# Square sums of a differential-attention entry: from 32 small TensorE products over eight tiles to sums on GpSimd and VectorE and 8 products

## The chip, the cores and the metric

One Trainium2 chip, one core. The metric is the device time of one execution in microseconds, the median of several runs. The core's engines work side by side and meet at semaphores: TensorE (PE in the profile, its weight loads PEld), VectorE (DVE), ScalarE (ACT), GpSimd (POOL) and SyncE (SP), which issues the transfers here.

## What is computed

Two transformer blocks of different kinds run one after the other on 512 tokens of width 1024, all in float32. The first ends in a norm, the second begins with one, and a differential attention follows:

```python
def rms_norm(x, g):
    y = xf * lax.rsqrt(jnp.mean(xf * xf, axis=-1, keepdims=True) + EPS)
    return (y * g.astype(jnp.float32)).astype(x.dtype)
...
    return rms_norm(x, final_norm)            # end of the first block
...
def rms_norm_2(x, g=None):                    # start of the second block
...
def diff_attention(h, w_in, q_g, k_g, ...):
    proj = h @ w_in
    q, k, v = jnp.split(proj, [2 * H * d, 4 * H * d], axis=-1)
    q = apply_partial_rope(rms_norm_2(q.reshape(B, S, 2 * H, d), q_g), cos, sin) * (d ** -0.5)
    k = apply_partial_rope(rms_norm_2(k.reshape(B, S, 2 * H, d), k_g), cos, sin)
...
```

The two norms in a row need two sums for each token: of x squared, and of (x times `final_norm`) squared. From them come two factors for each token: one by which the residual is scaled (first norm alone) and one for the rows of `h @ w_in` (both norms).

## The kernel before

Activations lie feature-major: `xT` is 8 tiles of 128 features x 512 tokens. Every large product is made of three float32r matmuls (`mm3`): weights and activations are each split into a high and a low part (`whi`, `wlo`; `hh`, `hl`), and high x high, high x low and low x high are added. Weights arrive in blocks of 128 x 2048 through three buffers. SyncE loads a block when TensorE has used the one three before it (`s_used`), ScalarE makes its high part (L952), GpSimd its low part in four instructions (`split_to`, L759).

Four engines run hand-written queues; their order is the order of the code. At the **entry** of the differential attention (stage `diff`, first block number b), for each tile t VectorE adds the last down-projection from PSUM to `xT` (L2362), ScalarE writes `hh` (L981, gain folded in) and the squares `a_xsq[:, t, :]` (L984), and VectorE writes `hl` (L2380). TensorE meanwhile works through the input projection with the tokens as rows: block b first (4 contraction tiles x 4 row tiles), then `half_group(b + 1, 0, 1, (0, 1))` and `half_group(b + 1, 0, 1, (2, 3))`, which finish group 0 of the rows. A half group of two row tiles is 24 large matmuls.

Before the change, TensorE also makes the token sums. `half_group` takes a function `between` that it calls ahead of each contraction tile; `squares` there issues 4 products of 2 columns, 32 in all, with a tile of `a_xsq` as the stationary operand and `gsq[:, t, :]` (ones, and the squared `final_norm`) as the moving one. The sums land in PSUM bank 7 with tokens on partitions. After the last one (`s_ess`) VectorE computes the factors `dr` (L2765 to L2772, with two ScalarE instructions for the inverse root between), and `s_rr` lets ScalarE copy group 0's rows out of PSUM (L1219, L1220).

The residual's factor is also needed as a row, the same on all partitions (`rstd`). For this VectorE builds four diagonal matrices (L2775) in `sq`, TensorE multiplies them by ones (L1951) in bank 6, and VectorE copies the result (L2792). That copy stands in VectorE's queue behind group 0's norm and rotation, and TensorE waits for it (`s_fcopy`) and for the rotated rows (`s_rows`) ahead of `turn_rows`, the 16 transposes of group 0 (L1901), which use banks 4 to 7.

## Time and profile before

| | us |
|---|---|
| median of 3 runs | 2386.46 |
| lowest, highest run | 2382.07, 2394.81 |
| span of the profiled execution | 2382.2 |
| TensorE busy | 2355.2 (99%) |
| GpSimd busy | 1162.4 (49%) |
| ScalarE busy | 853.5 (36%) |
| VectorE busy | 798.0 (33%) |

The profiled execution has no time of its own beside its span, which agrees with the fastest run to 0.1 us. TensorE's busy time is modelled for pipelined matmuls: a large matmul of 512 columns is shown as 0.39 us, though the next one starts 0.23 us after it. So starts are compared with starts below. A float32 product appears as two records, a float32r product or a transpose as one. An idle time in brackets names what ended it.

### The profile page before, as it was taken

The page shows a single profiled execution, that of the slowest core. Times are in us where ns is not written, and L with a number is a line of the kernel's source. Part 1 is how long each engine was busy: PE and PEld are TensorE (multiplying, and loading weights), DVE is VectorE, ACT ScalarE, POOL GpSimd, SP SyncE. Part 2 cuts the span into 40 slices and gives each one's busy share as a digit, 9 for nine tenths or more (in the row PEclk, how much of TensorE's full clock was granted, in tenths as well). Part 3 has the DMA queues.
Part 4 walks back from the last instruction along what each step waited for, and adds up shares of the span by engine and source line. Part 5 has one row for each costly group of instructions (what it writes and reads, how often), then busy time and mean ns, then how long its engine had stood idle before and what let it go on. Part 6 is the DMA issues. An engine that isn't in the chain of part 4 may idle for free.

```text
span 2382.2 us, 27151 instructions
## 1 busy us (share of the span) xinstructions
PE 2355.2 (99%) x11234; PEld 1924.9 (81%) x11234; DVE 798.0 (33%) x1384; ACT 853.5 (36%) x1266; POOL 1162.4 (49%) x960
## 2 busy tenths in 40 slices
PE   8999999999999999999999999999999999999999
PEld 7888887888887788888887678888887777788887
DVE  3222205854212322100466742022046863410210
ACT  4222214514342322212446543223156463431330
POOL 6544446634554544444452365444556822644443
PEclk9999999999999999999999999999999999999999
DMA  4323233212332323232220122233232201322322
GB/s 147 106 89 105 89 100 113 89 54 71 124 122 67 95 89 106 89 106 89 85 92 19 54 89 91 104 90 105 89 103 67 75 1 54 94 102 91 96 96 89
DMA packets 147521, 210.54 MB, mean 88 GB/s; under 512 B 6203, under 2 KB 113862, under 8 KB 147398
## 3 DMA queue, kind: packets, MB, share of 16 engines
q1 hardware_dynamic: 147398, 208.80, 27.2%
q8 instruction: 89, 1.46, 0.2%
q14 instruction: 34, 0.28, 0.0%
HBM read 206.69 MB, written 2.10 MB: 88 GB/s over the span
## 4 chain that ended last, share of the span: by engine, by line
PE 88%; DVE 7%; issue 2%; POOL 1%; DMA 1%; ACT 1%; SPq 0%; DVEq 0%; POOLq 0%; ACTq 0%
PE ps L1465 27%; PE ps L1467 26%; PE ps L1466 26%; PE ps L2243 2%; DVE c_work L2964 1%; DVE c_best L2963 1%; DVE small L2807 1%; PE ps L2221 1%; POOL wlo L759 1%; PE ps L2231 1%; PE ps L1726 1%; PE ps L1794 1%; POOL sq L774 1%; PE ps L1816 1%; DVE hl L2380 1%
## 5 line engine op out<-in xcount | busy, mean ns | idle before, releaser
L759 POOL TENSOR_TENSOR wlo<-raw,whi 128x512 fp32r<-128x512 f32 x776 | 1007.0, 1329 | 1082.9 <-ACT whi L952 981.8
L952 ACT ACTIVATE whi<-raw 128x2048 fp32r<-128x2048 f32 (+1 forms) x185 | 352.4, 1905 | 688.2 <-DMA raw<-in_mlp_w 317.1
L1465 PE MATMUL ps<-hh,whi 128*128 128x512 f32 x1448 | 572.9, 396 | 6.6 <-DVE hl L2380 5.4
L1467 PE MATMUL ps<-hh,wlo 128*128 128x512 f32 x1448 | 566.3, 391 | 0.0
L1466 PE MATMUL ps<-hl,whi 128*128 128x512 f32 x1448 | 566.3, 391 | 0.0
L1465 PEld LDWEIGHTS ps<-hh,whi 128*128 128x128 f32 x1448 | 273.5, 189 | 73.1 <-issue 9.3
L1467 PEld LDWEIGHTS ps<-hh,wlo 128*128 128x128 f32 x1448 | 273.3, 189 | 57.7
L1466 PEld LDWEIGHTS ps<-hl,whi 128*128 128x128 f32 x1448 | 273.7, 189 | 56.8 <-issue 1.2
L1466 PE MATMUL ps<-gl,whi 128*128 128x512 f32 x736 | 286.4, 389 | 0.0
L1465 PE MATMUL ps<-gh,whi 128*128 128x512 f32 x736 | 286.3, 389 | 0.0
L1467 PE MATMUL ps<-gh,wlo 128*128 128x512 f32 x736 | 286.3, 389 | 0.0
L2362 DVE SCALAR_TENSOR_TENSOR xT<-ps,xT 128x512 f32<-128x512 f32 x72 | 49.0, 684 | 479.3 <-PE ps L1467 479.3
L1466 PEld LDWEIGHTS ps<-gl,whi 128*128 128x128 f32 x736 | 138.1, 188 | 28.7
L1465 PEld LDWEIGHTS ps<-gh,whi 128*128 128x128 f32 x736 | 138.1, 188 | 28.7
L1467 PEld LDWEIGHTS ps<-gh,wlo 128*128 128x128 f32 x736 | 138.1, 188 | 28.6
L1465 PE MATMUL ps<-whi,hh 128*128 128x512 f32 (+2 forms) x408 | 154.5, 379 | 0.2 <-POOL wlo L759 0.2
L1467 PE MATMUL ps<-whi,hl 128*128 128x512 f32 (+2 forms) x408 | 151.4, 371 | 0.0
L1466 PE MATMUL ps<-wlo,hh 128*128 128x512 f32 (+2 forms) x408 | 151.3, 371 | 0.0
L2432 DVE SCALAR_TENSOR_TENSOR ps<-ps,rstd 128x512 f32<-128x512 f32 x64 | 41.5, 694 | 196.4 <-PE ps L1467 196.4
L1024 ACT ACTIVATE ps<-ps 128x512 f32<-128x512 f32 x64 | 37.1, 583 | 150.4 <-DVE ps L2432 150.0
L2417 DVE TENSOR_TENSOR ps<-ps,sg 128x512 f32<-128x512 f32 x44 | 28.5, 694 | 186.5 <-PE ps L1467 186.3
L1465 PEld LDWEIGHTS ps<-whi,hh 128*128 128x128 f32 x408 | 76.8, 188 | 14.5 <-POOL wlo L759 1.2
(448 smaller groups left out, 2920.1 us busy)
## 6 DMA issues: line engine op xcount, KB each, us to landing
raw<-in_mlp_w SPq DMA_DIRECT2D x64, 1024.0 KB, 5.5
raw<-in_ffn_w_up SPq DMA_DIRECT2D x22, 1024.0 KB, 5.1
raw<-in_ffn_w_down SPq DMA_DIRECT2D x22, 1024.0 KB, 4.8
raw<-in_ffn_w_gate SPq DMA_DIRECT2D x21, 1024.0 KB, 5.1
raw<-in_w_in SPq DMA_DIRECT2D x13, 1024.0 KB, 5.1
raw<-in_diff_w_in SPq DMA_DIRECT2D x12, 1024.0 KB, 5.0
raw<-in_xattn_w_kv SPq DMA_DIRECT2D x8, 1024.0 KB, 5.2
raw<-in_dsa_w_in SPq DMA_DIRECT2D x8, 1024.0 KB, 5.0
```

Of the source, the lines that this page charges most:

```text
L759: nc.gpsimd.tensor_tensor(wlo[i][:, c], raw[i][:, c], whi[i][:, c].bitcast(F32), ALU.subtract).then_inc(s_lo, 1)
L774: nc.gpsimd.tensor_tensor(sq[:, 0, :], first, sg[:, t % 4, :], ALU.add).then_inc(s_eacc, 1)
L952: nc.scalar.activation(whi[i][:, 0:width(made[0])], raw[i][:, 0:width(made[0])], ACT.Copy)\
L1024: nc.scalar.activation(ps[:, bank + n, :], ps[:, bank + n, :], ACT.Square)\
L1465: nc.tensor.matmul(dst, w_hi, x_hi, start=start, stop=False)
L1466: nc.tensor.matmul(dst, w_hi, x_lo, start=False, stop=False)
L1467: return nc.tensor.matmul(dst, w_lo, x_hi, start=False, stop=stop)
L1726: r = nc.tensor.matmul(ps[:, bank, ts(n, CH)], m_state[rows, d, h // 2, n, :], m_qin[rows, d, h // 2, ts(n, CH)], start=False, stop=d == 1 ...
L2243: r = nc.tensor.matmul(ps[:, 6, c:c + 64], c_pT[:, 2 * (p % 2) + a, ts(kb, P)], a_v[:, kb, ts(2 * j + a, 64)], start=kb == 0, stop=kb == qt)
L2362: V.scalar_tensor_tensor(out=xT[:, n, :], in0=ps[:, n, :], scalar=scale, in1=xT[:, n, :], op0=ALU.mult, op1=ALU.add).then_inc(s_x, 1)
L2417: dv.done(V.tensor_tensor(ps[:, bank + 2 + n, :], ps[:, bank + 2 + n, :], sg[:, (k0 + n) % 4, :], ALU.mult))
L2432: V.scalar_tensor_tensor(out=ps[:, bank + n, :], in0=ps[:, bank + n, :], scalar=0.0, in1=rstd[:, :], op0=ALU.max, op1=ALU.mult).then_inc(s ...
```

## The change

- GpSimd adds the eight tiles of `a_xsq` into `sq[:, 0, :]` with seven instructions, between its work on block b+1 and on block b+2.
- VectorE adds the same tiles, each times the squared gain of its features, into `sq[:, 1, :]` with eight instructions, each of which waits for the one before.
- `gsq` holds the squared gains alone, and `acc_at`, by which later entries count GpSimd's adds, counts the new seven too.
- TensorE waits for both and makes 8 products of 2 columns (4 row tiles x 2 sums) between the two half groups of block b+1, in place of the 32 inside the first one.
- The factor row comes from four TensorE transposes of a column of `dr`, broadcast along the free dimension, placed between block b+2 and block b+3. The four diagonals and the product with ones go away. VectorE's copy and TensorE's wait for it stay.

```diff
         def acc_at(e):
-            return 7 * (e - (e > E_DIFF))
+            return 7 * e
...
             def diff(b):
+                split_to(b + 1)
+                for t in range(1, KT):
+                    pool.wait_ge(s_esq, 8 * E_DIFF + t + 1)
+                    if t > 1:
+                        pool.wait_ge(s_eacc, acc_at(E_DIFF) + t - 1)
+                    first = a_xsq[:, 0, :] if t == 1 else sq[:, 0, :]
+                    nc.gpsimd.tensor_tensor(sq[:, 0, :], first, a_xsq[:, t, :], ALU.add).then_inc(s_eacc, 1)
                 split_to(b + DIFF_BLOCKS - 1)
...
                 pe.wait_ge(s_el, 8 * E_DIFF + 8)
-                pe.wait_ge(s_esq, 8 * E_DIFF + 8)
                 pe.wait_ge(s_x, x0 + 8)
-
-                def squares(st, k):
-
-                    row, part = divmod(4 * st + k, 2)
-                    for t in range(4 * part, 4 * part + 4):
-                        r = nc.tensor.matmul(ps[:, 7, 2 * row:2 * row + 2], a_xsq[:, t, ts(row, P)], gsq[:, t, :],
-                                             start=t == 0, stop=t == KT - 1)
-                    if row == ST - 1 and part:
-                        r.then_inc(s_ess, 1)
-
-                half_group(b + 1, 0, 1, (0, 1), squares)
+                half_group(b + 1, 0, 1, (0, 1))
+                pe.wait_ge(s_eacc, acc_at(E_DIFF) + 7)
+                pe.wait_ge(s_fsq, 1)
+                for st in range(ST):
+                    for n in range(2):
+                        r = nc.tensor.matmul(ps[:, 7, 4 * st + 2 * n:4 * st + 2 * n + 2], sq[:, n, ts(st, P)],
+                                             ones[:, 0:2], start=True, stop=True)
+                r.then_inc(s_ess, 1)
                 half_group(b + 1, 0, 1, (2, 3))
...
                 for g in range(1, 5):
                     half_group(b + 2 * g, 4 * g, 0)
+                    if g == 1:
+                        pe.wait_ge(s_rr, 1)
+                        for st in range(ST):
+                            r = nc.tensor.transpose(ps[:, 6, ts(st, P)], dr[:, st:st + 1].broadcast_to([P, P]),
+                                                    ident[:, :])
+                        r.then_inc(s_frow, 1)
                     half_group(b + 2 * g + 1, 4 * g, 1, (0, 1))
                     if g == 1:
-                        pe.wait_ge(s_fdiag, 4)
-                        nc.tensor.matmul(ps[:, 6, :], ones[:, :], sq[:, 0, :], start=True, stop=True)\
-                            .then_inc(s_frow, 1)
                         pe.wait_ge(s_fcopy, 1)
...
             def diff(b, upd, down):
+                for t in range(KT):
+                    dve.wait_ge(s_esq, 8 * E_DIFF + t + 1)
+                    if t == 0:
+                        last = V.tensor_scalar(sq[:, 1, :], a_xsq[:, 0, :], gsq[:, 0:1], None, ALU.mult)
+                    else:
+                        last = V.scalar_tensor_tensor(out=sq[:, 1, :], in0=a_xsq[:, t, :], scalar=gsq[:, t:t + 1],
+                                                      in1=sq[:, 1, :], op0=ALU.mult, op1=ALU.add)
+                    if t < KT - 1:
+                        dv.link(last)
+                last.then_inc(s_fsq, 1)
                 dve.wait_ge(s_ess, E_DIFF + 1)
...
-                dve.wait_ge(s_rr, 1)
-                for st in range(ST):
-                    V.tensor_scalar(sq[:, 0, ts(st, P)], ident[:, :], dr[:, st:st + 1], None, ALU.mult)\
-                        .then_inc(s_fdiag, 1)
```

TensorE at the end of block b and the start of b+1, before the change (`hh`, `hl` stationary or moving as the row says; `whi`, `wlo` the weights' parts, the number is the buffer's):

```order
L1467 MATMUL ps<-whi_58,hl 128x512
L1924 MATMUL ps<-gsq,a_xsq 128x2 [waits s_x,s_lo,s_esq,s_el]
L1924 MATMUL ps<-gsq,a_xsq 128x2 x3
L1465 MATMUL ps<-whi_59,hh 128x512
L1466 MATMUL ps<-wlo_56,hh 128x512
L1467 MATMUL ps<-whi_59,hl 128x512
L1924 MATMUL ps<-gsq,a_xsq 128x2 x4
```

The small products now stand together, 24 large matmuls later, between the halves of b+1 (`ones` is the moving operand):

```order
L1472 MATMUL ps<-whi_59,hh 128x512
L1473 MATMUL ps<-wlo_56,hh 128x512
L1474 MATMUL ps<-whi_59,hl 128x512
L1930 MATMUL ps<-ones,sq 128x2 [waits s_fsq,s_eacc]
L1930 MATMUL ps<-ones,sq 128x2 x7
L1472 MATMUL ps<-whi_59,hh 128x512 [waits s_lo]
```

They wait for two sums that were not there before, and the second half of b+1 stands behind them.

VectorE, from the end of the entry to the head sums of group 0, before:

```order
L2362 SCALAR_TENSOR_TENSOR xT<-ps,xT 128x512 [waits s_used]
L2380 SCALAR_TENSOR_TENSOR hl<-xT,g_90,hh 128x512 [waits s_eh] x2
L2765 TENSOR_SCALAR dr<-ps 128x4 [waits s_ess]
L2766 TENSOR_SCALAR newton<-ps 128x4
L2767 SCALAR_TENSOR_TENSOR dr<-dr,newton 128x4 [waits s_dv]
L2770 TENSOR_TENSOR newton<-dr 128x8 [waits s_erstd]
L2771 TENSOR_TENSOR dr<-dr,newton 128x8 [waits s_dv]
L2772 SCALAR_TENSOR_TENSOR dr<-dr 128x8 [waits s_dv]
L2775 TENSOR_SCALAR sq<-ident,dr 128x128 [waits s_rr]
L2775 TENSOR_SCALAR sq<-ident,dr 128x128 x3
L2757 TENSOR_REDUCE small<-a_sq 128x32 [waits s_rcopy,s_dv,s_rope]
```

And now:

```order
L2368 SCALAR_TENSOR_TENSOR xT<-ps,xT 128x512 [waits s_used]
L2386 SCALAR_TENSOR_TENSOR hl<-xT,g_90,hh 128x512 [waits s_eh] x2
L2771 TENSOR_SCALAR sq<-a_xsq,gsq 128x512 [waits s_esq]
L2773 SCALAR_TENSOR_TENSOR sq<-a_xsq,gsq,sq 128x512 [waits s_esq,s_dv] x7
L2780 TENSOR_SCALAR dr<-ps 128x4 [waits s_ess]
L2781 TENSOR_SCALAR newton<-ps 128x4
L2782 SCALAR_TENSOR_TENSOR dr<-dr,newton 128x4 [waits s_dv]
L2785 TENSOR_TENSOR newton<-dr 128x8 [waits s_erstd]
L2786 TENSOR_TENSOR dr<-dr,newton 128x8 [waits s_dv]
L2787 SCALAR_TENSOR_TENSOR dr<-dr 128x8 [waits s_dv]
L2762 TENSOR_REDUCE small<-a_sq 128x32 [waits s_rcopy,s_dv,s_rope]
```

The eight sums have come in ahead of the factors, and the four diagonals behind them are gone. Since the file is a few lines longer, line numbers behind a point move: L2380 is L2386 in the changed kernel, L2765 is L2780.

GpSimd in the changed kernel, where before the rows of L759 followed each other without a break:

```order
L759 TENSOR_TENSOR wlo_56<-raw_53,whi_59 128x512 [waits s_hi]
L759 TENSOR_TENSOR wlo_56<-raw_53,whi_59 128x512 x3
L862 TENSOR_TENSOR sq<-a_xsq 128x512 [waits s_esq]
L862 TENSOR_TENSOR sq<-sq,a_xsq 128x512 [waits s_eacc,s_esq] x6
L759 TENSOR_TENSOR wlo_57<-raw_54,whi_60 128x512 [waits s_hi]
```

The seven adds stand ahead of the low parts of block b+2.

## Rows read from the trace of the kernel before

**Rows 1.** Page, busy us, share of the span and instructions of an engine.

```profile
PE 2355.2 (99%) x11234; PEld 1924.9 (81%) x11234; DVE 798.0 (33%) x1384; ACT 853.5 (36%) x1266; POOL 1162.4 (49%) x960
```

**Rows 2.** Timeline of TensorE at the first small products: start, us, instructions.

```profile
1143.38 0.95 PE L1924 MATMUL ps<-gsq,a_xsq 128*128 128x2 f32 x8
1144.19 0.49 PE L1465 MATMUL ps<-whi,hh 128*128 128x512 f32 x1
...
1144.99 0.95 PE L1924 MATMUL ps<-gsq,a_xsq 128*128 128x2 f32 x8
```

**Rows 3.** Timeline of TensorE from the last cluster to group 0's transposes.

```profile
1156.09 0.40 PE L1465 MATMUL ps<-whi,hh 128*128 128x512 f32 x1
...
1177.88 1.02 PE L1951 MATMUL ps<-sq,ones 128*128 128x512 f32 x2
1179.69 1.97 PE L1901 MATMUL ps<-ident,a_rows 128*128 128x128 f32 x16 [0.78 <-DVE rstd L2792]
1181.41 0.47 PE L1465 MATMUL ps<-whi,hh 128*128 128x512 f32 x1
```

**Rows 4.** Timeline of VectorE from the entry to the copy of the factor row.

```profile
1130.85 1.10 DVE L2380 SCALAR_TENSOR_TENSOR hl<-xT,g,hh 128x512 fp32r<-128x512 f32 x1 [5.67 <-ACT hh L981]
...
1139.66 1.62 DVE L2380 SCALAR_TENSOR_TENSOR hl<-xT,g,hh 128x512 fp32r<-128x512 f32 x2
1155.49 0.16 DVE L2765 TENSOR_SCALAR dr<-ps 128x4 f32<-128x4 f32 x1 [14.21 <-PE ps L1924]
...
1178.24 0.42 DVE L2754 TENSOR_TENSOR a_rows<-t 128x256 f32<-128x256 f32 x1
1178.94 0.69 DVE L2792 COPY rstd<-ps 128x512 f32<-128x512 f32 x1 [0.28 <-PE ps L1951]
```

**Rows 5.** Timeline of GpSimd beside it: low parts of b+1 and b+2.

```profile
1128.85 5.95 POOL L759 TENSOR_TENSOR wlo<-raw,whi 128x512 fp32r<-128x512 f32 x4 [5.99 <-ACT whi L952]
1142.89 4.98 POOL L759 TENSOR_TENSOR wlo<-raw,whi 128x512 fp32r<-128x512 f32 x4 [8.10 <-ACT whi L952]
```

**Rows 6.** Timeline of VectorE at the third MLP pass's entry, first and last `hl`.

```profile
2022.59 1.09 DVE L2380 SCALAR_TENSOR_TENSOR hl<-xT,params,hh 128x512 fp32r<-128x512 f32 x1 [10.30 <-ACT hh L981]
...
2032.71 2.88 DVE L2380 SCALAR_TENSOR_TENSOR hl<-xT,params,hh 128x512 fp32r<-128x512 f32 x2
```

**Rows 7.** Timeline of GpSimd at that entry: low parts, then adds.

```profile
2020.60 5.94 POOL L759 TENSOR_TENSOR wlo<-raw,whi 128x512 fp32r<-128x512 f32 x4 [7.15 <-ACT whi L952]
...
2028.38 9.79 POOL L774 TENSOR_TENSOR sq<-sq,sg 128x512 f32<-128x512 f32 x6
```

**Rows 8.** All instructions of line L2380: ns min/median/max.

```profile
L2380 DVE SCALAR_TENSOR_TENSOR hl<-xT,params,hh x48: 733/1180/1785, 7.4 to 2033.8; 128x512 fp32r<-128x512 f32 x48
```

**Rows 9.** Timeline of VectorE in the first block's convolution, GpSimd idle.

```profile
516.11 0.54 DVE L2611 TENSOR_SCALAR m_conv<-m_u,params 128x512 f32<-128x512 f32 x1
516.68 0.75 DVE L2612 SCALAR_TENSOR_TENSOR m_conv<-m_u,params,m_conv 128x511 f32<-128x511 f32 x1
517.47 0.75 DVE L2614 SCALAR_TENSOR_TENSOR m_conv<-m_u,params,m_conv 128x511 f32<-128x511 f32 x1
```

**Rows 10.** Timelines of VectorE and GpSimd in the cross-attention's factors.

```profile
623.25 1.21 DVE L2352 SCALAR_TENSOR_TENSOR xqr<-xqr 128x4 f32<-128x4 f32 x1
624.49 1.22 DVE L2701 TENSOR_SCALAR xqr<-xqr 128x4 f32<-128x4 f32 x1
...
620.66 5.03 POOL L759 TENSOR_TENSOR wlo<-raw,whi 128x512 fp32r<-128x512 f32 x4 [2.08 <-ACT whi L952]
```

**Rows 11.** TensorE behind a long wait: stretches (busy, granted clock, DMA share, GB/s), then timeline.

```profile
1404.00:1407.00 3.00, 2.92 (x7) 0.50 0.00 0
1404.00:1410.00 6.00, 5.92 (x20) 0.75 0.00 0
...
1404.08 0.80 PE L1465 MATMUL ps<-hh,whi 128*128 128x512 f32 x1 [3.31 <-DVE hl L2380]
1404.67 0.63 PE L1466 MATMUL ps<-hl,whi 128*128 128x512 f32 x1
1405.10 0.63 PE L1467 MATMUL ps<-hh,wlo 128*128 128x512 f32 x1
```

More of the change, by code:

```diff
@@ L259, in two_blocks @@
         g12 = const("g12", [P, KT])
-        gsq = const("gsq", [P, KT, 2])
+        gsq = const("gsq", [P, KT])
         c_best = const("c_best", [P, 8])
@@ L452, in two_blocks @@
         s_dny = sem("s_dny")
-        s_fdiag = sem("s_fdiag")
+        s_fsq = sem("s_fsq")
         s_frow = sem("s_frow")
@@ L2474, in tables @@
                 at12, at1 = PARAM_AT["norm_mix_2"], PARAM_AT["final_norm"]
-                dv.done(V.memset(gsq[:, :, 0], 1.0))
-                dv.done(V.tensor_tensor(gsq[:, :, 1], params[:, at1:at1 + KT], params[:, at1:at1 + KT], ALU.mult))
+                dv.done(V.tensor_tensor(gsq[:, :], params[:, at1:at1 + KT], params[:, at1:at1 + KT], ALU.mult))
                 dv.done(V.tensor_tensor(g12[:, :], params[:, at12:at12 + KT], params[:, at1:at1 + KT], ALU.mult))
@@ L2762, in diff @@
             def diff(b, upd, down):
+                for t in range(KT):
[8 more added lines that the diff above has]
+                last.then_inc(s_fsq, 1)
                 dve.wait_ge(s_ess, E_DIFF + 1)
                 y, w, u = dr[:, 0:8], dr[:, 8:16], newton[:, 1, 0:8]
-                dv.done(V.tensor_scalar(w[:, 0:4], ps[:, 7, 0:8:2], -0.5 / D, -0.5 * EPS, ALU.mult, ALU.add))
-                dv.link(V.tensor_scalar(u[:, 0:4], ps[:, 7, 1:8:2], -0.5 / D, None, ALU.mult))
+                dv.done(V.tensor_scalar(w[:, 0:4], ps[:, 7, 0:16:4], -0.5 / D, -0.5 * EPS, ALU.mult, ALU.add))
+                dv.link(V.tensor_scalar(u[:, 0:4], ps[:, 7, 2:16:4], -0.5 / D, None, ALU.mult))
                 V.scalar_tensor_tensor(out=w[:, 4:8], in0=w[:, 0:4], scalar=EPS, in1=u[:, 0:4],
```

## Prediction

> **What bounds the kernel now.** I read the page first: TensorE is busy for 2355.2 of 2382.2 us [rows 1], so nearly every microsecond of this kernel is a TensorE microsecond. The change touches some 60 us around 1140 us, so the next views are the timelines of each engine there. I call the start of the square-sum products' reader on VectorE (the first `dr` instruction, L2765) the **handover**; it is at 1155.49 in the profile of before [rows 4].
>
> TensorE before the handover [rows 2]: eight clusters, each of eight records on L1924, then three large matmuls. From one cluster's start to the next takes 1144.99 - 1143.38 = 1.61 us, on the mean of all eight (1156.09 - 1143.38) / 8 = 1.59; the three large matmuls alone take 3 x 0.227 = 0.68 us (0.227 is the step through the 96 large matmuls from 1156.09 to 1177.88 in [rows 3]: 21.79 / 96). The code issues 32 products, four a cluster; the 64 of the change's title are records, two to a product. So "64 to 8" is 32 to 8 products, or 64 to 16 records.
>
> After the handover TensorE has more work than it needs to cover the row factors, but one place ties it to VectorE [rows 3, 4]: at 1177.88 it runs the ones-by-diagonal product (two records), VectorE copies `rstd` at 1178.94, and only then the 16 transposes of group 0 start, at 1179.69. VectorE reached that copy just in time: its last rotation instruction began at 1178.24 and took 0.42 us, so the copy could have begun at about 1178.70. From the handover to 1178.70 VectorE runs a chain of its own (factors, head sums, norm, rotation) of 23.2 us that the change leaves alone. **So what the change is worth is not what it takes off TensorE, but how far it moves the handover, plus the 1178.94 - 1178.70 = 0.24 us at the end.**
>
> **The parts, one by one.**
>
> *Removed on TensorE.* The clusters: 8 x (1.59 - 0.68) = 7.3 us. The ones-by-diagonal product and the wait behind it: 1179.69 - 1177.88 = 1.81 us [rows 3]. Four diagonal builds on VectorE lay in idle time and are worth nothing.
>
> *Added on TensorE.* 16 small records, at the pace of before's (8 in 1144.19 - 1143.38 = 0.81 us [rows 2]): 1.62 us at full clock. Four transposes: 16 take 1181.41 - 1179.69 = 1.72 us [rows 3], so 0.43, and 0.1 to get back to large matmuls: 0.55 us. They are placed 24 large matmuls ahead of the tie and wait for nothing late. A TensorE-only sum would be -7.3 - 1.8 + 1.7 + 0.55 = -6.8 us. The Trainium skill's page "TensorE: Matmul & The Clock Gate" (section "PE-mode transpose") gives about 275 ns for one 128x128 transpose in a kernel, which would make the four an estimated 1.1 us and the sum -6.1. The trace has them follow each other every 0.11 us, and the measurement decides.
>
> *Added on GpSimd: seven adds* of 128x512 behind the low parts of block b+1. GpSimd is idle there from 1134.80 (1128.85 + 5.95) to 1142.89 [rows 5], but VectorE is not: it writes `hl` and `xT`. The trace has the same arrangement once more, at the entry of the third MLP pass, where GpSimd also goes from four low parts straight to seven adds [rows 6, 7]. Its low parts end 3.95 us after the first `hl` instruction (2020.60 + 5.94 against 2022.59), as here (1134.80 against 1130.85, where `hl` of this entry begins). There VectorE's entry lasts 2032.71 + 2.88 - 2022.59 = 13.00 us; here it ends at 1139.66 + 1.62 = 1141.28, 10.43 us after its start [rows 4]. With the adds beside it I expect 13.00, an end at **1143.85**. The reason is in [rows 8]: `hl` instructions take 733 ns at best and 1785 at worst. The wait of TensorE for `hl` grows from nothing to 0.5 us (1143.38 to 1143.9); that is covered by what follows. GpSimd's adds end there 2028.38 + 9.79 - 2022.59 = 15.6 us after the start, so about two of them are still to come when VectorE leaves its entry, and behind them the four low parts of block b+2, whose high part ScalarE has by then. These low parts move from 1142.89 to past 1147, but TensorE wants them only after the remaining half of block b+1: covered.
>
> *Added on VectorE: eight dependent instructions* over `a_xsq`, begun only after its entry, and TensorE waits for the last. This is the costliest term. Undisturbed, the row for the first (tensor_scalar, SBUF, 128x512) is 0.54 us and for the others 0.79 from start to start (516.68 to 517.47) [rows 9]. Beside GpSimd they are slower: while GpSimd ran four low parts from 620.66 to 625.69, VectorE instructions on 128x4 elements took 1.2 us each, a tensor_scalar among them [rows 10]. So a VectorE instruction waits until GpSimd's current one is through. For 128x512 with two SBUF inputs the worst `hl`, 1.785 us [rows 8], is the last of a pair of 2.88 in [rows 6], whose starts are 1.09 apart; with 0.08 of overlap and 0.04 for the dependence I take **1.75 us a step**. GpSimd has 2 adds + 4 low parts left, so six steps are slow and two free: 6 x 1.75 + 2 x 0.79 = **12.1 us**, an end at 1143.85 + 12.1 = 1155.95. Bounds: none slow, 0.58 + 7 x 0.79 = 6.1 us; all eight slow, 14.0 us.
>
> The Trainium skill ("SBUF — State Buffer", section "Who interferes with whom") says that a VectorE instruction with two SBUF inputs and a GpSimd instruction that reads SBUF exclude each other for the whole instruction. By that rule a step would be a whole GpSimd instruction and a whole own one, an estimated 1.26 + 0.75 = 2.0 us in place of 1.75, and the result 1.5 us later; I keep the row. The rule speaks against this change.
>
> *The new wait and the clock.* TensorE has done the first half of block b+1 at 1143.9 + 24 x 0.227 = 1149.4 and then waits for VectorE until 1156.0, 6.6 us; behind that wait stand the small products, then the whole queue of large ones. In the profile of before, TensorE waited 3.31 us ahead of 1404.08, and over 1404 to 1407 the granted clock was 0.50, its lower level of 1.2 GHz: large matmuls came every 0.43 us (1404.67 to 1405.10) in place of 0.227, a factor of 1.9 [rows 11]. So I take the 16 small records at the lower clock: 1.62 x 1.9 = 3.1 us. The handover is then at 1155.95 + 0.05 + 3.1 + 0.05 = 1159.15, against 1155.49: **+3.65 us**.
>
> *Is VectorE still the later one at the tie?* From its large matmuls' resumption TensorE has 96 of them and four transposes, 21.8 + 0.55 = 22.3 us; VectorE needs 1179.69 - 0.24 - 1155.49 = 23.96 from handover to first transpose. The slack of 1.65 us swallows a few more large matmuls at the lower clock (seven cost 7 x 0.2 = 1.4). So the handover decides, and of TensorE's own 6.8 us nothing arrives.
>
> **Sum:** +3.65 - 0.24 = +3.4 us. The profiled execution has a span of 2382.2 us and lies at the fastest of the three runs (2382.07); with the change it would be 2385.6. Against the median of 2386.46 this gives **2390**. About 0.5% (12 us) is what a measurement of this kernel can tell from no change, so this is "no change", on the slow side.
>
> **Rivals.**
>
> A. *VectorE's sums don't collide with GpSimd* (for: undisturbed rows [rows 9]; against: [rows 8, 10]). End of sums 1143.85 + 6.1 = 1149.95, TensorE hardly waits, 1.62 us of products, handover 1151.7: -3.8 - 0.24 = -4.0, 2382.5. If even the tie were no limit, the TensorE-only sum of -6.8 would give 2379.7.
>
> B. *The collision is heavier*: all eight steps slow, 14.0 us (for: GpSimd may itself be slowed and so be busy longer; against: its own rows give six instructions left, [rows 7]). Handover 1.9 us later: +5.3, 2392. The Trainium skill's rule on the shared port (above) comes out here too, by its estimate.
>
> C. *The clock holds up* although TensorE waits: products 1.5 us shorter, +1.9, 2388.4. Against it: [rows 11].
>
> D. *Slower than before, measurably*: the wait of 6.6 us sends the clock down and it stays down through the 96 large matmuls, each 0.2 us longer: 19.2 less the slack of 1.65, +3.4 more, 21 us, 2407. It decides from about 50 large matmuls at the lower clock. Against it: in [rows 11] the low stretch had ended within 3 us of TensorE's resumption, since the mean of 1404 to 1410 is 0.75.
>
> E. *The change does not do what it says*: it saves TensorE products, but these were a filler that ran while VectorE's later chain was what counted. This is half true in my forecast; in full (handover unchanged) it gives -0.24, 2386.
>
> **How the numbers follow.** Chances: forecast 0.45, B 0.17, A 0.17 (0.04 of it with the tie gone), C 0.10, E 0.06, D 0.05. A to B reach from 2382.5 to 2392; the runs of before alone spread from 2382 to 2395, so a median of a few can lie some 3 us off: 2380 to 2396 leaves out D and the edges. Faster by over 0.5% needs -12 us, which no case gives, only the spread: 0.03. Slower by over 0.5%: D and a little spread, 0.06. Within: 0.91.
>
> **What would show it.** In the profile of the changed kernel: `hl` instructions of this entry at about 1.18 us throughout; the eight sums on VectorE at 1.6 to 1.8 us while GpSimd is busy and 0.75 after; a wait of TensorE of 5 to 8 us ahead of the small products, put down to VectorE, the largest in the kernel; a granted clock near 0.5 right behind it; the handover at 1157 to 1161; transposes of group 0 released by the `rstd` copy, with a wait of up to 1.7 us ahead. I am wrong if the sums take 0.8 us each beside GpSimd, if the wait is under 3 us, or if the time between handover and first transpose is not about 24 us.

## The result, and the profile after

| | before | after |
|---|---|---|
| median | 2386.11 us | 2389.99 us |
| lowest to highest | 2381.81 to 2394.81 | 2385.11 to 2393.36 |
| runs | 20 | 20 |

The ratio of the times is 1.0017, with a 95% interval of 1.0011 to 1.0024: the changed kernel is 3.9 us slower, which is real by its interval and below the half per cent that I called a difference. The forecast was 2390. The span of the profiled execution is 2387.6 us (2382.2 before). A few executions in the experiments, of before among others, took from about 3000 to 13000 us; the ratios leave them out, and the only profile of the kernel "new sums alone" is one of these, so it has no milestones below.

The page of after, engines, which answers to [rows 1]:

```profile
PE 2354.3 (99%) x11188; PEld 1921.2 (80%) x11188; DVE 810.7 (34%) x1387; ACT 854.0 (36%) x1266; POOL 1172.5 (49%) x967
```

TensorE has 46 instructions and 0.9 us of busy time less, and the kernel is slower. Where that comes from is in the timeline of VectorE (start, us, instructions; in brackets the idle time before and what ended it), which answers to [rows 4]:

```profile
1132.12 1.09 DVE L2386 SCALAR_TENSOR_TENSOR hl<-xT,g,hh 128x512 fp32r<-128x512 f32 x1 [5.55 <-ACT hh L988]
...
1142.27 2.88 DVE L2386 SCALAR_TENSOR_TENSOR hl<-xT,g,hh 128x512 fp32r<-128x512 f32 x2
1145.07 1.50 DVE L2771 TENSOR_SCALAR sq<-a_xsq,gsq 128x512 f32<-128x512 f32 x1
1146.61 9.97 DVE L2773 SCALAR_TENSOR_TENSOR sq<-a_xsq,gsq,sq 128x512 f32<-128x512 f32 x7
1160.30 0.16 DVE L2780 TENSOR_SCALAR dr<-ps 128x4 f32<-128x4 f32 x1 [3.73 <-PE ps L1930]
...
1169.99 2.29 DVE L2762 TENSOR_REDUCE small<-a_sq 128x32 f32<-128x2048 f32 x1 [8.18 <-ACT a_rows L1227]
...
1184.66 0.68 DVE L2803 COPY rstd<-ps 128x512 f32<-128x512 f32 x1
```

Beside it GpSimd, which answers to [rows 5] and [rows 7]. Six of the seven adds stand in one row, and the low parts of block b+2 behind them have no idle time ahead:

```profile
1136.04 1.74 POOL L862 TENSOR_TENSOR sq<-a_xsq 128x512 f32<-128x512 f32 x1
1137.92 9.81 POOL L862 TENSOR_TENSOR sq<-sq,a_xsq 128x512 f32<-128x512 f32 x6
1147.69 6.77 POOL L759 TENSOR_TENSOR wlo<-raw,whi 128x512 fp32r<-128x512 f32 x4
```

And TensorE, which answers to [rows 2] and [rows 3]:

```profile
1145.20 0.50 PE L1472 MATMUL ps<-whi,hh 128*128 128x512 f32 x1 [0.32 <-DVE hl L2386]
...
1156.72 3.54 PE L1930 MATMUL ps<-ones,sq 128*128 128x2 f32 x16 [5.75 <-DVE sq L2773]
1160.13 0.77 PE L1472 MATMUL ps<-whi,hh 128*128 128x512 f32 x1
...
1165.39 0.63 PE L1472 MATMUL ps<-whi,hh 128*128 128x512 f32 x1
1165.82 0.44 PE L1473 MATMUL ps<-wlo,hh 128*128 128x512 f32 x1
...
1179.27 0.60 PE L1954 MATMUL ps<-ident,dr 128*128 128x128 f32 x4
...
1185.40 1.97 PE L1908 MATMUL ps<-ident,a_rows 128*128 128x128 f32 x16
```

The stretches around TensorE's wait (busy, granted clock, DMA share, GB/s) show how long the lower clock lasted:

```profile
1152.00:1155.00 3.00, 0.00 (x0) 1.00 0.00 0
1155.00:1158.00 3.00, 1.27 (x7) 0.61 0.00 0
1158.00:1161.00 3.00, 3.00 (x13) 0.50 0.02 5
1161.00:1164.00 3.00, 3.00 (x8) 0.50 0.00 0
1164.00:1167.00 3.00, 3.00 (x10) 0.68 0.00 0
```

For all kernels I use the same two milestones, both counted from the first `hl` of the entry (1130.85 before, 1132.12 after), so that what happened earlier in an execution drops out: the handover (VectorE's first `dr` instruction) and the first of group 0's 16 transposes, behind which the code is the same again. The last two columns are the shift of the transposes against before, and the ratio of the times to those of before in the same comparison, with its 95% interval.

| kernel | handover | transposes | shift | ratio |
|---|---|---|---|---|
| before | 24.64 | 48.84 | | |
| after | 28.18 | 53.28 | +4.44 | 1.0017 [1.0011, 1.0024] |
| after, once more | 28.19 | 53.37 | +4.53 | 1.0022 [1.0013, 1.0031] |
| low parts after the sums | 22.98 | 48.49 | -0.35 | 1.0001 [0.9992, 1.0010] |
| low parts after the factors | 23.00 | 47.54 | -1.30 | 1.0003 [0.9994, 1.0012] |
| TensorE's wait filled | 26.64 | 50.64 | +1.80 | 1.0008 [1.0000, 1.0017] |
| low parts after the factors, wait filled | 23.03 | 47.60 | -1.24 | 0.9991 [0.9982, 1.0001] |
| no adds on GpSimd | 19.97 | 44.52 | -4.32 | 0.9990 [0.9981, 0.9999] |
| new factor row alone | 24.63 | 48.48 | -0.36 | 0.9994 [0.9985, 1.0003] |
| new row, old products in one piece | 23.89 | 54.00 | +5.16 | 1.0016 [1.0006, 1.0026] |
| new sums alone | none | none | | 1.0026 [1.0016, 1.0036] |
| half sums, 4 clusters | 24.07 | 49.25 | +0.41 | 1.0014 [1.0003, 1.0026] |
| half sums, 6 clusters | 22.23 | 46.83 | -2.01 | 0.9990 [0.9980, 0.9999] |
| before, clusters twice as large | 23.86 | 48.70 | -0.14 | 0.9993 [0.9984, 1.0003] |

The milestones come from one execution each. "After" was run twice, and its two rows agree to 0.1 us. The medians are noisier: the difference of two medians lies up to 3 us from the shift of the milestones (before with larger clusters: -3.1 us by the median, -0.14 by the milestone). So a step of a microsecond is read from the milestones, and the medians say only whether the sum of it all is there.

### The profile page after: what moved, and what is told of

The parts are those of the page before. It is cut to its first block, busy times and chain, and to the rows that moved or that the text cites. A ratio compares the mean times of both kernels' runs of the same rounds, so it can differ in the third digit from the quotient of the medians.

```text
span 2387.6 us, 27082 instructions
## 1 busy us (share of the span) xinstructions
PE 2354.3 (99%) x11188; PEld 1921.2 (80%) x11188; DVE 810.7 (34%) x1387; ACT 854.0 (36%) x1266; POOL 1172.5 (49%) x967
## 4 chain that ended last, share of the span: by engine, by line
PE 85%; DVE 9%; issue 2%; DMA 1%; POOL 1%; ACT 1%; SPq 0%; DVEq 0%; POOLq 0%; ACTq 0%
PE ps L1472 26%; PE ps L1474 26%; PE ps L1473 26%; PE ps L2249 2%; DVE c_work L2975 1%; DVE c_best L2974 1%; DVE hl L2386 1%; DVE small L2818 1%; PE ps L2227 1%; POOL wlo L759 1%; PE ps L2237 1%; PE ps L1801 1%; POOL sq L774 1%; PE ps L1823 1%; PE ps L1733 1%
## 5 line engine op out<-in xcount | busy, mean ns | idle before, releaser
L759 POOL TENSOR_TENSOR wlo<-raw,whi 128x512 fp32r<-128x512 f32 x776 | 1006.4, 1330 | 1079.0 <-ACT whi L959 978.4
```

What stands on the lines that cost most here:

```text
L759: nc.gpsimd.tensor_tensor(wlo[i][:, c], raw[i][:, c], whi[i][:, c].bitcast(F32), ALU.subtract).then_inc(s_lo, 1)
```

## The experiments

My theory had two parts: VectorE's sums are slow because GpSimd works beside them, and the wait that this makes on TensorE lowers its clock for the small products. The rivals were that the sums are as long as they are by themselves, that the clock costs nothing that reaches the end, and that the new factor row, not the sums, moves the time.

### GpSimd's low parts after VectorE's sums

```diff
                     nc.gpsimd.tensor_tensor(sq[:, 0, :], first, a_xsq[:, t, :], ALU.add).then_inc(s_eacc, 1)
+                pool.wait_ge(s_fsq, 1)
                 split_to(b + DIFF_BLOCKS - 1)
```

> The changed kernel, with one wait more: GpSimd begins the low parts of block b+2 only when VectorE's eight sums are through. Theory (VectorE's sums wait for GpSimd's instructions): only the last two adds are left beside the sums, so two of eight steps are slow (1.5 to 1.8 us) and six take 0.79; the sums last about 7.9 us in place of 11.5, TensorE waits some 2 us in place of 5.7, its clock stays at 1.00, the 16 small records take 1.7 us, the handover comes 2.0 us earlier than in the kernel before, measured from the entry's first hl, and the time is 2 us below the kernel before (ratio 0.999). Rival (the sums are slow by themselves, through the dependence from one to the next): they stay at 11.5 us and the kernel stays 4 us above (1.0017).

Timeline of VectorE, then of GpSimd, in this kernel:

```profile
1141.86 1.51 DVE L2772 TENSOR_SCALAR sq<-a_xsq,gsq 128x512 f32<-128x512 f32 x1
1143.40 6.39 DVE L2774 SCALAR_TENSOR_TENSOR sq<-a_xsq,gsq,sq 128x512 f32<-128x512 f32 x7
...
1152.91 0.73 DVE L2786 TENSOR_TENSOR newton<-dr 128x8 f32<-128x8 f32 x1 [0.52 <-ACT dr L981]
1153.67 1.20 DVE L2787 TENSOR_TENSOR dr<-dr,newton 128x8 f32<-128x8 f32 x1
```

```profile
1149.87 4.98 POOL L759 TENSOR_TENSOR wlo<-raw,whi 128x512 fp32r<-128x512 f32 x4 [5.35 <-DVE sq L2774]
```

The seven steps fall from 9.97 to 6.39 us, with nothing of VectorE's changed: the collision is real and is made in good part by the low parts. The sum shows its size as well. Once GpSimd's last adds are done a step is free at 0.79 us [rows 9], so, if one of these seven is slow, it takes 6.39 - 6 x 0.79 = 1.65 us, 0.86 more than a free one. With that price after's 9.97 us hold (9.97 - 7 x 0.79) / 0.86 = 5.2, about 5 slow steps and 2 free ones; the eighth instruction, the first of the sum, was slow too, 1.50 us against 0.54 [rows 9].

The handover came 5.2 us earlier than in after, and 1.66 earlier than before. At the transposes only 0.35 of it was left. The two lower rows tell where it went: the postponed low parts now ran beside the factors, and two instructions on 8 columns took 0.73 and 1.20 us. So a collision cost about as much here on 8 columns (1.20 - 0.17 = 1.03 us) as on 512 (0.86 us); moving GpSimd's work moves the place where it is paid. The 2 us expected did not come (ratio 1.0001), and the clock, expected at 1.00, fell behind the small products here too, to 0.50 from 1153 to 1156.

### GpSimd's low parts after the factors

```diff
+                pool.wait_ge(s_rr, 1)
                 split_to(b + DIFF_BLOCKS - 1)
```

> The changed kernel, whole, with the low parts of block b+2 held back until the factors are computed, not only until the sums are (there, the two small factor instructions took 0.73 and 1.20 us beside them in place of 0.17). Theory (VectorE waits for whatever GpSimd runs): sums 7.9 us as in that run, factor instructions at 0.17 again, handover 1.7 us earlier than before the change, the transposes of group 0 1.9 earlier, if TensorE's wait for the low parts of b+2 (due about 1 us after TensorE has ended block b+1) stays inside its slack; time 1.9 us below the kernel before (0.9992). Rival (the low parts now come too late, and TensorE's low clock behind its wait takes the rest): transposes no earlier than before, ratio 1.000 to 1.001.

Timeline of TensorE, then of VectorE:

```profile
1149.98 1.92 PE L1931 MATMUL ps<-ones,sq 128*128 128x2 f32 x16 [2.21 <-DVE sq L2774]
...
1176.47 1.97 PE L1909 MATMUL ps<-ident,a_rows 128*128 128x128 f32 x16 [0.58 <-DVE rstd L2804]
```

```profile
1152.87 0.17 DVE L2786 TENSOR_TENSOR newton<-dr 128x8 f32<-128x8 f32 x1 [0.52 <-ACT dr L981]
```

The factors are at 0.17 us an instruction again, the handover is where the last experiment had it, and the transposes come 0.95 us earlier than there. That confirms the last reading. The kernel is before's equal, no more: the median (2386.21 against 2386.12) shows nothing of the 1.30 us, which is within what medians scatter. It is also less than the 1.9 us expected. 0.4 us of that is the clock again: it fell behind the small products (0.50 from 1153 to 1156), ScalarE's fourth copy waited 0.29 us for TensorE, and the head sums began 8.61 us after the handover, against 8.21 before.

### TensorE's wait filled

```diff
                 half_group(b + 1, 0, 1, (0, 1))
+                for _ in range(25):
+                    nc.tensor.matmul(ps[:, 6, :], hh[:, 0, 0:P], whi[(b + 1) % NBUF][:, 0:S], start=True, stop=True)
```

> The changed kernel, with 25 large matmuls into an unused PSUM bank put between the first half of block b+1 and the wait for the sums, 5.7 us of work whose result nobody reads. Theory (the wait sends TensorE's clock down, and that costs as much as the late sums): clock 1.00 throughout, 16 small records in 1.7 us in place of 3.4, handover 1.8 us earlier, head sums of group 0 another 1.2 earlier, since the second half of b+1 is at full clock; the time is about 3 us below the changed kernel, 1 us above the kernel before (ratio 1.0004). Rival (the small products are slow because their operand was just written, the clock has no part in it): they stay at 3.4 us and the time stays 4 us above.

Timeline of TensorE, and a stretch behind the small products:

```profile
1156.73 1.92 PE L1932 MATMUL ps<-ones,sq 128*128 128x2 f32 x16 [0.18 <-DVE sq L2775]
```

```profile
1159.00:1162.00 3.00, 3.00 (x9) 0.50 0.00 0
```

25 large matmuls whose result nobody reads turn an idle TensorE into a busy one. The sums end at the same time; the small products take 1.92 us in place of 3.54, the handover comes 1.54 us earlier and the transposes 2.64 us. So of after's shift of +4.44 us, **at least 2.64 are the clock's**. The remaining 1.80 are the late sums', less what the factor row gains, and a little of the clock is still in them. For the clock did not stay at 1.00 throughout, as expected: behind the small products it fell here too, for some eight large matmuls in place of 13, and the head sums began 8.60 us after the handover, against 8.21 before and 9.69 in after. The clock's part is larger than what it takes from the small products: 1.1 us of what the filler gave back lies behind the handover, where the forecast had let it vanish in slack.

### Both together

```diff
                 half_group(b + 1, 0, 1, (0, 1))
+                for _ in range(9):
+                    nc.tensor.matmul(ps[:, 6, :], hh[:, 0, 0:P], whi[(b + 1) % NBUF][:, 0:S], start=True, stop=True)
...
+                pool.wait_ge(s_rr, 1)
                 split_to(b + DIFF_BLOCKS - 1)
```

> As e7_low_after_factors, with 9 large matmuls (2.0 us) whose result nobody reads in TensorE's remaining wait for the sums. Theory (the wait, not the small products, sends the clock down, here 1 us after the products have ended): clock 1.00 through block b+1, and if the low clock had cost e7 anything, this kernel is up to 1.6 us faster; else the same, since VectorE's copy is what the transposes wait for. Rival (16 small records in 1.8 us lower the clock by themselves): the same low stretch of 3 us as there.

Timeline of TensorE, and the stretch behind it:

```profile
1152.86 1.92 PE L1933 MATMUL ps<-ones,sq 128*128 128x2 f32 x16 [0.17 <-DVE sq L2776]
```

```profile
1156.00:1159.00 3.00, 3.00 (x9) 0.53 0.00 0
```

A miss. With the wait filled to 0.17 us the clock should have held and the transposes should have come earlier than with the wait of 2.21 us; they stand at 47.60 against 47.54. In both the small products ran at full clock (1.92 us) and the clock fell behind them: here to 0.53, there, in the stretch from 1153, to 0.50. So with the wait filled the clock held through the small products, but in neither of the two filled kernels beyond them. The fall came behind 16 small records and a wait of 0.17 us; the next experiments bear on that.

### No adds on GpSimd, and no low parts beside the sums

The seven adds are taken out, and both sums are read from the weighted one, so this kernel leaves out the plain sum.

```diff
-                for t in range(1, KT):
...
-                    nc.gpsimd.tensor_tensor(sq[:, 0, :], first, a_xsq[:, t, :], ALU.add).then_inc(s_eacc, 1)
+                pool.wait_ge(s_rr, 1)
                 split_to(b + DIFF_BLOCKS - 1)
...
-                        r = nc.tensor.matmul(ps[:, 7, 4 * st + 2 * n:4 * st + 2 * n + 2], sq[:, n, ts(st, P)],
+                        r = nc.tensor.matmul(ps[:, 7, 4 * st + 2 * n:4 * st + 2 * n + 2], sq[:, 1, ts(st, P)],
                                              ones[:, 0:2], start=True, stop=True)
```

> The changed kernel without GpSimd's seven adds, and with its low parts of block b+2 held back until the factors are through, so that GpSimd does nothing beside VectorE from the middle of the entry to the factors. The plain sums are left out (all 8 products read the weighted sums). Theory (collisions with GpSimd are what turned the gain into a loss): counted from the entry's first hl, the entry lasts 10.4 us as before the change (13.0 in the changed kernel), the sums 6.1 (11.5), TensorE doesn't wait, its clock stays up, the handover is at 19.8 us (24.6 before, 28.2 changed), group 0's transposes at 43.8 (48.8 before, 53.3 changed); the time is 5 us below the kernel before (ratio 0.9979). Rival (the sums are slow by themselves or a wait elsewhere takes the gain): handover later than 24, ratio 1.000 or above.

Timeline of VectorE, then of TensorE, and the stretch behind the small products:

```profile
1141.45 0.48 DVE L2765 TENSOR_SCALAR sq<-a_xsq,gsq 128x512 f32<-128x512 f32 x1
1141.97 5.47 DVE L2767 SCALAR_TENSOR_TENSOR sq<-a_xsq,gsq,sq 128x512 f32<-128x512 f32 x7
```

```profile
1149.20 1.84 PE L1924 MATMUL ps<-ones,sq 128*128 128x2 f32 x16
...
1157.76 0.50 PE L1467 MATMUL ps<-whi,hh 128*128 128x512 f32 x1 [1.10 <-POOL wlo L759]
...
1175.63 1.97 PE L1903 MATMUL ps<-ident,a_rows 128*128 128x128 f32 x16 [0.75 <-DVE rstd L2797]
```

```profile
1150.00:1153.00 3.00, 3.00 (x19) 1.00 0.00 0
```

With GpSimd idle the same eight instructions take 1141.97 + 5.47 - 1141.45 = 6.0 us in place of 11.5, TensorE does not wait for them, and the transposes are 4.32 us earlier than before and 8.76 earlier than in after. This is the rival A of the forecast, made true (it said -4.0 us): had nothing collided, the handover would have come early. The postponed low parts of b+2 are now late for TensorE, by 1.10 us, but that did not reach the transposes, where TensorE still waited 0.75 us for VectorE. The expectation had them at 43.8 us, 0.7 us too early.

### The factor row alone, and the products in one piece

The first kernel is before with the new factor row. The second also issues the 32 old products in one piece ahead of the half group, in place of eight clusters.

```diff
-                        pe.wait_ge(s_fdiag, 4)
-                        nc.tensor.matmul(ps[:, 6, :], ones[:, :], sq[:, 0, :], start=True, stop=True)\
-                            .then_inc(s_frow, 1)
...
+                    if g == 1:
+                        pe.wait_ge(s_rr, 1)
+                        for st in range(ST):
+                            r = nc.tensor.transpose(ps[:, 6, ts(st, P)], dr[:, st:st + 1].broadcast_to([P, P]),
+                                                    ident[:, :])
+                        r.then_inc(s_frow, 1)
```

> The kernel before with the factor row alone changed: four transposes behind block b+2 in place of four diagonals and the product with ones; the 32 products stay. Theory (VectorE's chain from the handover to the copy sets the time at the transposes of group 0): the transposes start 0.24 us earlier, the time is the same within the measurement (ratio 0.9999). Rival (TensorE's own work sets it): 1.81 - 0.55 = 1.3 us less, 0.9995.

Timeline of TensorE with the new row alone:

```profile
1180.81 1.97 PE L1900 MATMUL ps<-ident,a_rows 128*128 128x128 f32 x16 [0.84 <-DVE rstd L2790]
```

-0.36 us at the transposes, where I had 0.24 from [rows 4]. The copy now begins 0.33 us after the start of the last rotation instruction (1180.07 and 1179.74), against 0.70 before (1178.94 and 1178.24); I had let it wait for that instruction's end. TensorE waits 0.84 us for the copy, because its own saving reaches nobody. The factor row is a small gain and no cause of the loss.

```diff
-                half_group(b + 1, 0, 1, (0, 1), squares)
+                for i in range(8):
+                    squares(i // 4, i % 4)
+                half_group(b + 1, 0, 1, (0, 1))
```

> The kernel before with the factor row by transposes, and the 32 small products in one piece ahead of block b+1 in place of eight clusters inside its first half. Theory: 64 records take 6.5 us from 1143.4, so the handover comes 5.6 us earlier; VectorE is then early at group 0's transposes and TensorE's own work sets them: 6.5 + 0.1 + 120 x 0.227 + 0.55 us after 1143.4, that is 1177.8 against 1179.69, 1.9 us less (ratio 0.9992). Rival (the handover sets all): 5.8 us less (0.9976). Second rival (the records are no cheaper in one piece and e3's saving is nothing): same.

Timeline of TensorE, and three stretches:

```profile
1145.04 11.41 PE L1923 MATMUL ps<-gsq,a_xsq 128*128 128x2 f32 x64
```

```profile
1145.00:1148.00 3.00, 3.00 (x27) 0.91 0.48 121
1148.00:1151.00 3.00, 3.00 (x16) 0.50 0.59 229
...
1157.00:1160.00 3.00, 3.00 (x9) 0.50 0.00 0
```

This was to show how little the place of the products matters, and showed the opposite. 64 records at 0.1 us each should take 6.5 us; they took 11.41, since the clock fell to 0.50 within 3 us **while TensorE was never idle**. The handover is early (23.89), and yet the transposes come 5.16 us late, because the half group of large matmuls that used to lie between the clusters now lies behind them, in part at the lower clock.

### The new sums with the old factor row

```diff
-                        pe.wait_ge(s_rr, 1)
-                        for st in range(ST):
-                            r = nc.tensor.transpose(ps[:, 6, ts(st, P)], dr[:, st:st + 1].broadcast_to([P, P]),
...
+                        pe.wait_ge(s_fsq, 5)
+                        nc.tensor.matmul(ps[:, 6, :], ones[:, :], sq[:, 0, :], start=True, stop=True)\
+                            .then_inc(s_frow, 1)
```

> The changed kernel with the old factor row: sums on GpSimd and VectorE and 8 products, but four diagonals and the product with ones. In the changed kernel TensorE came to group 0's transposes 0.1 us after VectorE's copy. Theory: with the product with ones ahead of the copy again, the transposes start about 1.2 us later than in the changed kernel, 5.6 later than in the kernel before; ratio 1.0022. Rival (the factor row is worth 0.3 us as when done alone): 1.0018.

The ratio is 1.0026; with the new row (after, in two comparisons) it is 1.0017 and 1.0022. The intervals overlap. Its median of 2391.87 lies 1.9 us above after's, the way that the row's gain points, but no milestone bears it out. What the run does show is that the sums alone carry the whole loss; how much the row gives back on top of them stays open.

### Half the sums on TensorE

Here GpSimd and VectorE add only the first four tiles (three adds, four weighted steps), the low parts wait for the factors, and TensorE takes the other four tiles with the two partial sums in 24 products. The first kernel issues them in four clusters of 12 records ahead of the fourth to seventh of the half group's eight contraction steps, the second in six clusters of 8 ahead of the second to seventh.

```diff
-                for t in range(1, KT):
+                for t in range(1, 4):
...
+                def squares(st, k):
+                    row = 4 * st + k - 3
...
+                    for t in range(4, KT):
+                        nc.tensor.matmul(ps[:, 7, 2 * row:2 * row + 2], a_xsq[:, t, ts(row, P)], gsq[:, t, :],
+                                         start=t == 4, stop=False)
+                    for n in range(2):
+                        r = nc.tensor.matmul(ps[:, 7, 2 * row:2 * row + 2], sq[:, n, ts(row, P)], gsq[:, n, :],
+                                             start=False, stop=n == 1)
...
-                half_group(b + 1, 0, 1, (0, 1))
+                half_group(b + 1, 0, 1, (0, 1), squares)
```

> A middle way built on what the runs so far showed. GpSimd and VectorE add only tiles 0 to 3 (3 adds, 4 sums); TensorE adds the two partial sums and tiles 4 to 7 itself with 24 products in place of 32 or 8, in four clusters between the large matmuls of block b+1's first half; GpSimd's low parts of block b+2 wait until the factors are through; factor row by four transposes. Theory (collisions, and small products in one piece, cost more than the saved products bring): counted from the entry's first hl, the entry ends at 11.7 us, the sums at 14.8, the clock stays at 1.00, the handover is at 22.1 (24.6 before, 28.2 changed), group 0's transposes at 45.9 (48.8, 53.3); the time is 2.9 us below the kernel before (ratio 0.9988). Rival (TensorE's clock falls here too, or the low parts of b+2 come too late): transposes no earlier than 47.5, 0.9995 or above.

Timeline of TensorE at the first, third and fourth cluster, and a stretch:

```profile
1143.55 0.39 PE L1476 MATMUL ps<-whi,hl 128*128 128x512 f32 x1
1143.95 1.02 PE L1938 MATMUL ps<-gsq,a_xsq 128*128 128x2 f32 x8
...
1148.10 0.95 PE L1938 MATMUL ps<-gsq,a_xsq 128*128 128x2 f32 x8
...
1150.76 1.70 PE L1938 MATMUL ps<-gsq,a_xsq 128*128 128x2 f32 x8
```

```profile
1150.00:1153.00 3.00, 3.00 (x15) 0.50 0.00 0
```

The sums ended almost in time: the first cluster starts 0.40 us behind the last large matmul in place of 0.23, a wait of 0.17 us. The clock was still at 1.00 through the third cluster and fell to its lower level behind it: eight records of the third took 0.95 us, of the fourth 1.70. The second kernel has the same products, in smaller portions:

```diff
-                    row = 4 * st + k - 3
+                    step = 4 * st + k - 1
...
+                    for j in range(4 * step, 4 * step + 4):
+                        r = product(*divmod(j, 6))
```

> As e10_half_sums, with its 24 small products (48 records) in six clusters of eight records, one ahead of each contraction tile's three large matmuls from the second on, as the kernel before spaces them, in place of four clusters of twelve with gaps of 0.83 us. Theory (e10 lost its gain because its denser clusters brought TensorE's clock down): clock 1.00, handover 22.1 us after the entry's first hl (24.1 in e10, 24.6 before), group 0's transposes at 45.9 (49.3, 48.8); time 2.9 us below the kernel before (ratio 0.9988). Rival (the clock falls whenever small products stand there before the factors, or something else sets the transposes): 48 or later, ratio 1.000.

Its timeline of VectorE, whose entry began at 1129.60, and the same stretch:

```profile
1141.79 2.33 DVE L2793 SCALAR_TENSOR_TENSOR sq<-a_xsq,gs,sq 128x512 f32<-128x512 f32 x3
1151.83 0.17 DVE L2800 TENSOR_SCALAR dr<-ps 128x4 f32<-128x4 f32 x1 [7.71 <-PE ps L1934]
```

```profile
1150.00:1153.00 3.00, 3.00 (x19) 1.00 0.00 0
```

Here the clock holds at 1.00, the three weighted steps take 2.33 us since GpSimd is idle by then, and the transposes come 2.01 us before before's. The median is 2382.91 us against 2385.83 in the same comparison, and the ratio 0.9990 [0.9980, 0.9999]: the only complete kernel of the study whose interval lies below one, and that barely, in one comparison out of thirteen. In this kernel nothing waited ahead of the first cluster, so it differs from the first one by the portions and by that wait of 0.17 us, and the two kernels don't tell which of them kept the clock.

### Before, with clusters twice as large

```diff
+                def pairs(st, k):
+                    if k % 2 == 0:
+                        squares(st, k)
+                        squares(st, k + 1)
+
-                half_group(b + 1, 0, 1, (0, 1), squares)
+                half_group(b + 1, 0, 1, (0, 1), pairs)
```

> The kernel before with its 32 small products in four clusters of sixteen records, six large matmuls between, in place of eight clusters of eight with three between: the same work in coarser pieces. If the share of small work decides whether TensorE's clock holds (half here, as before): clock 1.00, handover at 23.9 us after the entry's first hl (24.6 before, since the last cluster comes two large steps sooner), time the same. If the length of a piece decides: the clock falls to 0.50 for 3 us or more, as in e10, and the handover is at 25 or later.

Timeline of TensorE at the second of the four clusters, and a stretch at the third and behind it:

```profile
1143.84 1.84 PE L1924 MATMUL ps<-gsq,a_xsq 128*128 128x2 f32 x16
```

```profile
1147.00:1150.00 3.00, 3.00 (x23) 1.00 0.00 0
```

16 records at a time with six large matmuls between them hold the clock, where 12 at a time with three between them lost it. The handover is where it was expected (23.86 for 23.9). So it is not the length of a single cluster that decided here. Here too nothing waited ahead of the clusters. Each of these three readings of the clock is from one execution; the medians of the two kernels with half sums (2386.56 and 2382.91) lie apart the same way.

### After, once more

Unchanged, beside the first kernel of the half sums.

> The changed kernel as it is, beside e10_half_sums on the same chip: transposes of group 0 at 53.3 us from the entry's first hl, ratio 1.0017 (1.001 to 1.0025). If this profile differs from the first one by more than 0.5 us in that span, the spans of single profiles are not fit to be compared as they were.

TensorE waited 5.75 us for the sums again, and both milestones came out within 0.1 us of the first profile's.

## Why the prediction was right, and which step of it failed

Times again from the first `hl`.

| step | predicted | measured |
|---|---|---|
| VectorE's entry with the adds beside it | 13.00 | 13.03 |
| TensorE's wait for `hl` | 0.5 | 0.32 |
| eight sums | 12.1 | 11.5 |
| TensorE's wait for them | 6.6 | 5.75 |
| 16 small records at the lower clock | 3.1 | 3.41 |
| shift of the handover | +3.65 | +3.54 |
| handover to transposes | 23.96 | 25.10 |
| shift of the transposes | +3.4 | +4.44 |
| median | 2390 | 2389.99 |

Each step in this table up to the shift of the handover came out near its forecast. The time from the handover to the transposes did not: the forecast had named "not about 24 us" there as a sign of being wrong, and it was 25.10.

**The entry.** Taking the whole duration from the third MLP pass [rows 6, 7] was right to 0.03 us: 1142.27 + 2.88 - 1132.12. The same two engines did the same work side by side there, and a row of a like place is worth more than a sum of single prices.

**The sums.** About six slow steps and two free ones, as forecast; a slow one costs some 1.65 us (1.50 the first), not 1.75. GpSimd's rows show that the loss is mutual: its four low parts behind the adds took 6.77 us, against 4.98 undisturbed [rows 5]. The rule of the Trainium skill ("SBUF — State Buffer", "Who interferes with whom"), that the two exclude each other for a whole instruction, is borne out in kind by the adds taken away (6.0 us for 11.5) and by the 8-column instruction that took 1.20 us; the estimate of 2.0 us a step that the forecast worked out from it was too high, and the 1.65 of the runs stands.

**The wait and the clock.** TensorE's wait was put down to VectorE's sum, as the waits of the trace say (releaser, then total, count, longest):

```profile
PE ps L1930 <- DVE sq L2773: 5.7, 1, 5.7
```

It is the longest single wait of the kernel, as forecast, and 0.85 us shorter than forecast, 0.6 of which is the sums'. The clock fell as in [rows 11], and the filler shows it to be the cause of the longer products: 1.92 us without the fall.

**The step that failed** is "the slack of 1.65 us swallows a few more large matmuls at the lower clock (seven cost 1.4)". Both halves of it were off. The clock stayed low for 13 large matmuls, from 1160.13 to 1165.8, each 0.43 us in place of 0.227: 2.6 us, where [rows 11] had led me to allow 1.4. That is 0.95 more than the slack, and TensorE reached the transposes by itself only at 1185.40. And the slack was reckoned at the wrong place. On its way to them VectorE's chain also needs TensorE once before: ScalarE's copy of group 0's last row tile waits for the second half of block b+1, which stands right behind the small products and was slowed most. In before that copy began at 1162.28 without a wait. Timeline of ScalarE in after:

```profile
1168.59 0.69 ACT L1226 ACTIVATE a_sq<-ps,dr 128x512 f32<-128x512 f32 x1 [1.37 <-PE ps L1474]
```

The head sums, which wait for that copy, began 1169.99 - 1160.30 = 9.69 us after the handover, against 8.21 before. So VectorE's `rstd` copy (1184.66) ended at 1185.34, just when TensorE arrived: two paths, both made late by the clock, met. From the head sums on, the chain took 15.41 us against 15.99. 0.35 of that is the factor row's, since with the new row alone it took 15.64. Another 0.21 is the first small instruction behind the head sums, in before and in after:

```profile
1166.02 0.39 DVE L2346 TENSOR_SCALAR newton<-small 128x32 f32<-128x32 f32 x1
```

```profile
1172.31 0.18 DVE L2352 TENSOR_SCALAR newton<-small 128x32 f32<-128x32 f32 x1
```

In before it ended with GpSimd's low parts of the next block, which ran from 1161.34 to 1166.37; in after those began at 1166.14 and were done by 1171.20. So the shift of the transposes adds up: 3.54 + (9.69 - 8.21) - (15.99 - 15.41) = 4.44 us.

The median came out on the forecast to 0.01 us by luck: the forecast carried +3.4 where the milestones say +4.44 and the medians +3.9, which differ by what single executions and medians scatter, and it was added to a median of three runs that lay 0.35 us above that of twenty.

**The rivals.** A, no collision: refuted by the steps themselves, and the kernel without adds shows what it would have given. B, all steps slow: no, two were free. C, the clock holds: refuted (0.50). D, it stays low: refuted, it was back by 1166. E, the handover doesn't move: false, +3.54.

## What to carry to other kernels

Work that is taken off the busiest engine is worth only what the chain that it feeds gains: here TensorE gave up 7.3 us of products, and the sums in their place were 11.5 us of dependent VectorE work beside a busy GpSimd, with TensorE waiting at their end. Before moving sums to VectorE, look at what GpSimd has queued in that stretch, and move its later instructions past the whole dependent chain, small instructions included, not only past the large ones. A wait on TensorE is paid again behind its end, at every place up to the next tie where another engine needs TensorE's result; in these kernels small products did best in small portions between large matmuls, without a wait ahead of them.

## What the runs showed of the hardware that I had not expected

- The granted clock can fall to 0.50 without any idle time: 64 records of 2 columns in one piece started at full clock and were at 0.50 within 3 us, and took 11.41 us for an expected 6.5.
- The clock went with how small products are portioned, in one profiled execution each: clusters of 12 records with three large matmuls between them fell to 0.50 (eight records took 1.70 us for 0.95), clusters of 8 with three between, and of 16 with six between, stayed at 1.00. Only the first had a wait, of 0.17 us, ahead of its clusters.
- What stays open: behind the same 16 small records the clock stayed at 1.00 in the kernel without adds, which had no wait ahead of them, and fell to its lower level in both kernels with filler, which had a rest of 0.17 or 0.18 us of wait, and in both with the low parts postponed, which had 2.2 us. That even a rest of wait makes the difference is only a guess, and the half sums fit it as well as they fit the portions; no run separated the two.
- A VectorE instruction on 128x8 elements took 1.20 us beside GpSimd, whose instructions there took 4.98 / 4 = 1.25 us each, and 0.17 us without: what it paid was near a GpSimd instruction, not its own length.
